# A two-layer trunk with top-2 experts: gates applied at the expert's eviction, and gathers that add into the residual

## The chip, the cores and the metric

One core of one Trainium2 chip. The metric is the device time of one execution in microseconds (us), the median of several runs. The engines are TensorE (PE, matrix products and transpositions), VectorE (DVE), ScalarE (ACT), GpSimd (POOL) and SyncE (SP); transfers run on 16 DMA engines. ACTq, POOLq and SPq are the queues on which ScalarE, GpSimd and SyncE issue their transfers.

## What is computed

The reference is a trunk of two layers on 512 tokens of width 1024, in float32. Layer 0 mixes with a causal convolution, layer 1 with sliding-window attention; both end with a mixture of 16 experts, of which each token takes two. The part that matters here:

```python
def deepnorm(x, sub, g, b):
    return layer_norm(DEEPNORM_ALPHA * x + sub, g, b)

# in grouped_moe: two experts a token, their gates normalised to 1
gate = jnp.take_along_axis(aff, expert, axis=1)
gate = gate / gate.sum(-1, keepdims=True)
...
yb = lax.map(expert_block, (xb, blk_expert)).reshape(P, D)
y = jnp.zeros_like(xt).at[tok_buf].add(yb * gate_buf[:, None].astype(yb.dtype))

# the layer
x = deepnorm(x, mix, ln_g[layer, 0], ln_b[layer, 0])
ffn = grouped_moe(x, router_w, router_b, moe_w_gate[layer], moe_w_up[layer], moe_w_down[layer])
x = deepnorm(x, ffn, ln_g[layer, 1], ln_b[layer, 1])
```

## The kernel before

The 512 tokens are four tiles (T = 4) of 128 rows, held in SBUF as `x_sb`. Each engine has its own program; they meet at semaphores.

**Routing.** For each tile VectorE's `route` chooses two experts and reads their affinities into `gatev`; it signals `s_mask`, and the PE counts ranks (`rank_products`). VectorE's `places` makes of them two row numbers a token (`place_i`, signal `s_place`). After the last tile `table` says how many blocks of 64 rows beyond the first each expert has (`extra`, `s_extra`), and computes all normalised gates, `gate_w`, in three small instructions behind that signal. GpSimd's `scatter(l, t)` (L1507) writes the tile's activations to `xs_dram`, a table of 16 x 512 rows in HBM, with two indirect DMAs of 128 rows of 4 KB. In layer 0 the scatters of tiles 0 and 1 stand in GpSimd's order before the inverse deviations of the normalisation of tiles 2 and 3 (L1570 to L1575); in layer 1 the scatters of tiles 0 and 1 stand behind those of tiles 2 and 3 (L1587 to L1594).

**Experts.** GpSimd waits for all scatters, then fetches 64 rows an expert, four DMAs of 64 KB (`fetch`). The PE runs for each expert e a gate product, an up product, a transposition and a down product, in an order that overlaps e with e - 1 (`step`). SyncE streams the weights, 2 MB each, into six slots; a load waits until the PE has begun the next expert. ScalarE evicts the down product from PSUM with a copy (`store`, L1294) and writes it to `xs_dram`, at the place where the activations were. At the start of the stage ScalarE multiplies `x_sb` by the constant ALPHA (`s_xal`).

**Combine.** GpSimd waits for all stores, and for each tile gathers the two rows of each token (L1561) into two buffers of the tile, `yg[t][0]` and `yg[t][1]`, two indirect DMAs of 512 KB, all eight in one go but for two inverse deviations. ScalarE multiplies the first by its gates (`gated_y`, L1348); VectorE multiplies the second by its gates and adds it to `x_sb` (L1070), adds the first (L1073), and normalises the tile (`norm_x`): moments (L862, L864), subtraction and scale (L882), then, with GpSimd's inverse deviation (`inverse_std`, L1504 and L1505), the rest (L885). VectorE takes tile by tile. In layer 1 the tiles then go to the output.

**Between the layers.** SyncE waits for all eight gathers of layer 0 (L427 and L428) before it loads the two halves of the query weights, then those of the output product, each 2 MB. The PE's first units of attention are the transpositions of tile 0, its KV product, and Q0 and Q1 (L700); VectorE evicts them behind its four normalisations (L1115 to L1126), in its program's order.

The functions `combine` and `scatter` run once a layer. In the convolution stage there is one tile of normalisation after the other, and the routing of a tile follows the normalisation of the next.

## Time and profile before

| | us |
|---|---|
| median of 3 runs | 1238.12 |
| lowest and highest | 1235.01 and 1239.14 |
| the profiled execution | 1231.42 |
| its span in the trace | 1229.8 |

| busy | us | share of the span |
|---|---|---|
| PE | 974.5 | 79% |
| DVE | 493.2 | 40% |
| POOL | 241.2 | 20% |
| ACT | 167.9 | 14% |

In time: the convolution and its routing last to about 312 us, the experts of layer 0 from 324 to 601, the combine of layer 0 from 605 to 642, attention and its routing to about 894, the experts of layer 1 from 908 to 1181, the last combine from 1185 to 1222. In the expert stages the DMA engines are busy nine tenths of the time or more, in the combines the PE is idle.

A busy share is an average over these stages. The order of time (the timeline) shows for each instruction when it starts, how long it takes, and in brackets how long its engine was idle before it and what released it. For a transfer the row is its issue; that it has landed is seen at the instruction that waited for it.

### The profile page before, as it was taken

What the parts mean: (1) busy time and instruction counts of PE and PEld (TensorE: products, weight loads), DVE (VectorE), ACT (ScalarE), POOL (GpSimd) and SP (SyncE); (2) the same over time, 40 slices, a digit from 0 to 9 for tenths busy, and PEclk for the clock granted to TensorE, in tenths of its full rate; (3) what the DMA queues carried; (4) which work ended last, traced back from release to release, by engine and by line L of the source; (5) the groups of instructions that cost most, each with busy time, mean ns of one, the idle gap of its engine ahead of it and who ended that gap; (6) DMA issues with size and microseconds to landing.
All of it is one profiled execution on the core that took longest, in us unless ns stands there. A gap on an engine that the chain in (4) does not pass through costs nothing.

```text
span 1229.8 us, 14566 instructions
## 1 busy us (share of the span) xinstructions
PE 974.5 (79%) x5112; PEld 509.8 (41%) x5113; DVE 493.2 (40%) x967; ACT 167.9 (14%) x375; POOL 241.2 (20%) x335
## 2 busy tenths in 40 slices
PE   5999597996498969899578899967549778999930
PEld 3444243454354435454234454534335334445510
DVE  1799993365211101111185566575511111111126
ACT  0000002120100000000112323433010000000010
POOL 1254500011421202110151002021141121121022
PEclk8999798987699989999888999988769897999975
DMA  9999711025589999999782001300559999999952
GB/s 294 402 402 405 297 69 68 1 103 197 195 322 386 365 385 393 383 341 399 275 289 111 1 1 69 137 1 18 240 195 344 378 393 390 371 399 331 398 183 102
DMA packets 76668, 308.46 MB, mean 251 GB/s; under 512 B 7101, under 2 KB 15465, under 8 KB 68296
## 3 DMA queue, kind: packets, MB, share of 16 engines
q1 hardware_dynamic: 40368, 226.50, 48.5%
q10 hardware_dynamic: 26136, 53.19, 11.6%
q0 software_dynamic: 10112, 28.06, 6.7%
q8 instruction: 34, 0.56, 0.2%
q14 instruction: 18, 0.15, 0.0%
HBM read 252.41 MB, written 55.31 MB: 250 GB/s over the span
## 4 chain that ended last, share of the span: by engine, by line
PE 53%; DMA 21%; DVE 10%; issue 9%; POOL 3%; ACT 2%; SPq 0%; DVEq 0%; ACTq 0%; POOLq 0%
PE ps L581 17%; DMA wring<-in_moe_w_up_dram 9%; PE ps L591 9%; DMA wring<-in_moe_w_gate_dram 8%; PE ps L700 5%; PE ps L526 5%; PE ps L719 5%; PE ps L500 5%; DVE arena L843 2%; DMA wring<-in_conv_w_dram 1%; PE ps L488 1%; DMA xs_dram<-x_sb,place_i 1%; PE ps L745 1%; PE ps L757 1%; POOL vareps L1504 1%
## 5 line engine op out<-in xcount | busy, mean ns | idle before, releaser
L581 PE MATMUL ps<-wring,arena 128*64 128x256 f32 x2624 | 316.1, 398 | 77.0 <-DMA wring<-in_moe_w_gate_dram 32.1
L581 PEld LDWEIGHTS ps<-wring,arena 128*64 128x64 f32 x2624 | 196.5, 144 | 197.8 <-issue 103.1
L1519 POOL DMA_DIRECT2D arena<-xs_dram x172 | 92.0, 535 | 374.4 <-DVE arena L1002 340.3
L591 PE MATMUL ps<-wring,arena 128*64 128x512 f32 x688 | 155.6, 594 | 6.8 <-DVE arena L1037 5.7
L843 DVE SCALAR_TENSOR_TENSOR arena<-arena,dwT 128x512 f32<-128x512 f32 (+1 forms) x174 | 125.4, 798 | 0.0
L488 PE MATMUL ps<-arena,wring 128*128 128x512 f32 x256 | 112.7, 602 | 9.9 <-DMA wring<-in_conv_w_dram 9.6
L1023 DVE COPY arena<-ps 128x256 f32<-128x256 f32 x32 | 13.6, 425 | 258.0 <-PE ps L626 258.0
L700 PE MATMUL ps<-wring,arena 128*128 128x512 f32 x192 | 88.6, 617 | 6.8 <-DMA wring<-in_attn_wq_dram 3.4
L591 PEld LDWEIGHTS ps<-wring,arena 128*64 128x64 f32 x688 | 48.6, 137 | 87.5 <-issue 74.9
L488 PEld LDWEIGHTS ps<-arena,wring 128*128 128x128 f32 x256 | 49.2, 193 | 72.0 <-issue 72.0
L1504 POOL TENSOR_SCALAR vareps<-mv 128x1 f32<-128x1 f32 x20 | 21.2, 1061 | 267.1 <-DVE mv L864 267.0
L500 PE MATMUL ps<-arena,wring 128*128 128x512 f32 x124 | 55.4, 609 | 12.9 <-DVE arena L828 12.9
L526 PE MATMUL ps<-wring,arena 128*128 128x512 f32 x128 | 60.4, 629 | 2.1 <-ACT arena L1255 1.5
L1002 DVE STREAM_TRANSPOSE arena<-arena 128x512 f32<-128x512 f32 x43 | 47.4, 1103 | 33.4 <-DMA arena<-xs_dram 25.7
L719 PE MATMUL ps<-wring,arena 128*128 128x512 f32 x128 | 60.2, 626 | 0.0
L700 PEld LDWEIGHTS ps<-wring,arena 128*128 128x128 f32 x192 | 37.1, 198 | 51.9 <-issue 50.8
L1017 DVE TENSOR_TENSOR arena<-arena,ps 128x256 f32<-128x256 f32 x32 | 13.5, 421 | 101.1 <-PE ps L581 101.1
L1294 ACT ACTIVATE arena<-ps 128x512 f32<-128x512 f32 x32 | 19.1, 597 | 237.7 <-PE ps L591 237.7
L500 PEld LDWEIGHTS ps<-arena,wring 128*128 128x128 f32 x124 | 24.1, 195 | 44.2 <-issue 30.4
L1561 POOL DMA_INDIRECT arena<-xs_dram,place_i x16 | 17.5, 1093 | 119.7 <-DMA xs_dram<-arena 115.7
L1035 DVE TENSOR_TENSOR arena<-arena,ps 128x256 f32<-128x256 f32 x11 | 4.6, 421 | 88.5 <-PE ps L581 88.5
L526 PEld LDWEIGHTS ps<-wring,arena 128*128 128x128 f32 x128 | 25.4, 203 | 32.3 <-issue 30.5
(181 smaller groups left out, 859.1 us busy)
## 6 DMA issues: line engine op xcount, KB each, us to landing
wring<-in_moe_w_up_dram SPq DMA_DIRECT2D x32, 2048.0 KB, 17.5
wring<-in_moe_w_down_dram SPq DMA_DIRECT2D x32, 2048.0 KB, 14.3
wring<-in_moe_w_gate_dram SPq DMA_DIRECT2D x30, 2048.0 KB, 10.2
xs_dram<-zero ACTq DMA_DIRECT2D x1, 32768.0 KB, 105.7
arena<-xs_dram POOLq DMA_DIRECT2D x172, 64.0 KB, 7.3
xs_dram<-arena ACTq DMA_DIRECT2D x86, 128.0 KB, 7.9
wring<-in_conv_w_dram SPq DMA_DIRECT2D x8, 1024.0 KB, 11.4
wring<-in_conv_w_dram SPq DMA_DIRECT2D x2, 2048.0 KB, 17.4
```

Source lines behind the costliest of these rows:

```text
L488: last = pe.matmul(ps[:, 2 * (c % 4) + h, :], w[:, k, h, (c % 2) * P:(c % 2) * P + P], xT[:, k, :], start=(k == 0), stop=(k == KD - 1))
L500: last = pe.matmul(ps[:, 2 * (c % 4) - 4, :], diag(c)[:, k, :], hpad[:, c, k:k + S], start=(k == 0), stop=(k == CW - 1))
L526: last = pe.matmul(ps[:, 4 + h, :], hc[t % 2][:, c, :], slot(4 + c // 4, 4)[:, c % 4, h * 512:(h + 1) * 512], start=(c == 0), stop=(c == K ...
L581: mm = pe.matmul(ps[h * CAP:(h + 1) * CAP, bank, 0:256], act[:, k, :], w[:, k, h * 256:(h + 1) * 256], start=(k == 0), stop=(k == KD - 1))
L591: mm = pe.matmul(ps[h * CAP:(h + 1) * CAP, bank, :], act[:, j % 2, (j // 2) * CAP:(j // 2 + 1) * CAP], w[:, j, h * 512:(h + 1) * 512], sta ...
L700: last = pe.matmul(ps[:, bank, :], xTt[:, k, :], slot(at, KD)[:, k, :], start=(k == 0), stop=(k == KD - 1))
L719: last = pe.matmul(ps[:, bank, :], oT[t % 2][:, k, :], slot(3 + h, KD)[:, k, :], start=(k == 0), stop=(k == KD - 1))
L843: dve.scalar_tensor_tensor(out=acc, in0=hpad[:, one, k:k + S], scalar=dwT[:, one, k:k + 1], in1=acc, op0=ALU.mult, op1=ALU.add).then_inc(s ...
L1002: return dve.transpose(xgT[i].rearrange("p k (h c) -> p h k c", h=2), xg[i].rearrange("p h (c k) -> p h k c", k=KD))
L1294: act.activation(ysb[b], ps[:, 4, :], ACT.Copy).then_inc(s_yc, 1)
L1504: own(pool.tensor_scalar(vareps[:, n:n + 1], mv[:, n, 1:2], EPS, None, ALU.add))
L1519: pool.dma_start(where[q * QROWS:(q + 1) * QROWS, :, :], xs_tiles[q, :, bass.ds(n, 1), :, :]).then_inc(signal, 16)
```

## The change

The gates are applied to the experts' products instead of to the gathered rows. To have them in the order of the places, they are written to a table `gate_dram` of 16 x 512 floats by the same row numbers (two more indirect DMAs a tile, of one float for each of 128 partitions); the table is read back as 128 blocks of 64 twice, side by side (`gate2`), and turned by the PE into `gateT`, with a column for each block. ScalarE's eviction of the down product takes that column as its scale. For the scatters, the gates are normalised tile by tile in `route`.

In the combine, VectorE and ScalarE no longer multiply. For tile 0 the first row's gather adds into `x_sb`, and the second goes to a buffer that VectorE adds. For tiles 1 to 3 both gathers add into `x_sb`, the second issued when the first has landed. SyncE's wait before the query weights counts two gathers for tile 0 and one for each of the others.

```diff
@@ block.sync
             for t in range(T):
-                sp.wait_ge(s_yg[t], 32)
+                sp.wait_ge(s_yg[t], 32 if t == 0 else 16)
@@ block.tensor, experts
                 stage_u(0, 0, 0, False)
+                pe.wait_ge(s_gtab, 32 * (l + 1))
+                pe.transpose(ps[:, 0, 0:P], gate2[:, :, :].rearrange("p h s -> p (h s)"), ident[:, :]).then_inc(s_gT, 1)
                 extras(0, 0, 0)
@@ block.vector, route (and the same for all tiles out of table)
                 own(dve.tensor_reduce(gatev[:, :, t], r3[:, :, :], AX.X, ALU.add))
+                own(dve.tensor_tensor(gsum[:, t:t + 1], gatev[:, 0, t:t + 1], gatev[:, 1, t:t + 1], ALU.add))
+                own(dve.reciprocal(gsum[:, t:t + 1], gsum[:, t:t + 1]))
+                dve.tensor_scalar(gate_w[:, :, t], gatev[:, :, t], gsum[:, t:t + 1], None, ALU.mult).then_inc(s_gw, 1)
@@ block.vector, combine
-                dve.wait_ge(s_xal, T * (l + 1))
+                dve.wait_ge(s_yg[0], 32 * (l + 1))
+                dve.tensor_tensor(x_sb[:, 0, :], x_sb[:, 0, :], y_first, ALU.add).then_inc(s_cmb, 1)
+                dve.wait_ge(s_cmb, l + 1)
                 for t in range(T):
-                    y0, y1 = yg[t]
                     dve.wait_ge(s_yg[t], 32 * (l + 1))
-                    own(dve.scalar_tensor_tensor(out=x_sb[:, t, :], in0=y1, scalar=gate_w[:, 1, t:t + 1],
-                                                 in1=x_sb[:, t, :], op0=ALU.mult, op1=ALU.add))
-                    dve.wait_ge(s_y0g, T * l + t + 1)
-                    dve.tensor_tensor(x_sb[:, t, :], x_sb[:, t, :], y0, ALU.add).then_inc(s_cmb, 1)
-                    dve.wait_ge(s_cmb, T * l + t + 1)
                     norm_x(t, n + t, l, 1)
@@ block.scalar: store (extras alike), experts
-                    act.activation(ysb[b], ps[:, 4, :], ACT.Copy).then_inc(s_yc, 1)
+                    act.activation(ysb[b], ps[:, 4, :], ACT.Copy, scale=gateT[:, bass.ds(e * NBLK, 1)]).then_inc(s_yc, 1)
...
                 silu(0, 0, False)
+                act.wait_ge(s_gT, l + 1)
+                act.activation(gateT[:, :], ps[:, 0, 0:P], ACT.Copy).then_inc(s_gTc, 1)
+                act.wait_ge(s_gTc, l + 1)
...
-            def gated_y(l, t):
-
-                y0 = yg[t][0]
-                act.wait_ge(s_yg[t], 32 * (l + 1))
-                act.activation(y0, y0, ACT.Copy, scale=gate_w[:, 0, t:t + 1]).then_inc(s_y0g, 1)
-
@@ block.gpsimd, scatter
+                if l == 0 and t == 0:
+                    pool.wait_ge(s_ginit, 16)
+                pool.wait_ge(s_gw, T * l + t + 1)
+                for j in range(2):
+                    pool.indirect_dma_start(out=gate_dram[:, :],
+                                            out_offset=bass.IndirectOffsetOnAxis(ap=place_i[:, j, t:t + 1], axis=0),
+                                            in_=gate_w[:, j, t:t + 1], in_offset=None).then_inc(s_gscat, 16)
@@ block.gpsimd, experts
                 gather(1, 1, False)
+                pool.wait_ge(s_gscat, 16 * 2 * T * (l + 1))
+                for h in range(2):
+                    pool.dma_start(gate2[:, h, :], gate_tiles).then_inc(s_gtab, 16)
                 pool.wait_ge(s_extra, l + 1)
@@ block.gpsimd, combine
-                for t in range(T):
-                    for j in range(2):
-                        pool.indirect_dma_start(out=yg[t][j], out_offset=None, in_=xs_dram[:, :],
-                                                in_offset=bass.IndirectOffsetOnAxis(ap=place_i[:, j, t:t + 1], axis=0)
-                                                ).then_inc(s_yg[t], 16)
-                    if t >= 2:
-                        inverse_std(n + t - 2)
-                for t in range(T - 2, T):
-                    inverse_std(n + t)
+                pool.wait_ge(s_xal, T * (l + 1))
+                def collect(t, j, into, how):
+
+                    pool.indirect_dma_start(out=into, out_offset=None, in_=xs_dram[:, :],
+                                            in_offset=bass.IndirectOffsetOnAxis(ap=place_i[:, j, t:t + 1], axis=0),
+                                            compute_op=how).then_inc(s_yg[t], 16)
+
+                collect(0, 0, x_sb[:, 0, :], ALU.add)
+                collect(0, 1, y_first, ALU.bypass)
+                for t in range(1, T):
+                    collect(t, 0, x_sb[:, t, :], ALU.add)
+                for t in range(1, T):
+                    pool.wait_ge(s_yg[t], 32 * l + 16)
+                    collect(t, 1, x_sb[:, t, :], ALU.add)
+                    inverse_std(n + t - 1)
+                inverse_std(n + T - 1)
```

In layer 0 `gate_dram` is set to zero beside `xs_dram`, by one DMA on ScalarE's queue ahead of that one.

## Rows read from the trace of the kernel before

**Rows 1.** The page's chain that ended last, shares of the span by engine.

```profile
PE 53%; DMA 21%; DVE 10%; issue 9%; POOL 3%; ACT 2%; SPq 0%; DVEq 0%; ACTq 0%; POOLq 0%
```

**Rows 2.** Timeline, combine of layer 1: start, us, engine, line, operation [idle before <-releaser].

```profile
1185.04 1.04 POOL L1561 DMA_INDIRECT arena<-xs_dram,place_i  x1 [57.76 <-DMA xs_dram<-arena]
...
1191.38 0.93 POOL L1561 DMA_INDIRECT arena<-xs_dram,place_i  x1 [0.30 <-issue]
...
1191.67 1.28 DVE L1070 SCALAR_TENSOR_TENSOR x_sb<-arena,gate_w,x_sb 128x1024 f32<-128x1024 f32 x1 [14.83 <-DMA arena<-xs_dram,place_i]
...
1197.68 1.15 ACT L1348 ACTIVATE arena<-arena,gate_w 128x1024 f32<-128x1024 f32 x1 [1.35 <-DMA arena<-xs_dram,place_i]
...
1204.96 1.15 ACT L1348 ACTIVATE arena<-arena,gate_w 128x1024 f32<-128x1024 f32 x1 [6.13 <-DMA arena<-xs_dram,place_i]
...
1206.67 1.28 DVE L1070 SCALAR_TENSOR_TENSOR x_sb<-arena,gate_w,x_sb 128x1024 f32<-128x1024 f32 x1
...
1214.13 1.28 DVE L1070 SCALAR_TENSOR_TENSOR x_sb<-arena,gate_w,x_sb 128x1024 f32<-128x1024 f32 x1
...
1220.38 1.28 DVE L885 SCALAR_TENSOR_TENSOR x_sb<-x_sb,rstd,lnrow 128x1024 f32<-128x1024 f32 x1 [0.83 <-POOL rstd L1505]
```

**Rows 3.** Timeline, end of the combine of layer 0 and start of attention.

```profile
621.99 8.88 PE L700 MATMUL ps<-wring,arena 128*128 128x512 f32 x16 [0.73 <-issue]
...
625.42 0.56 SPq L429 DMA_DIRECT2D wring<-in_attn_wq_dram  x1
...
634.25 13.97 PE L700 MATMUL ps<-wring,arena 128*128 128x512 f32 x32 [3.38 <-DMA wring<-in_attn_wq_dram]
...
642.36 0.41 DVE L1115 TENSOR_TENSOR arena<-ps,rows 128x256 f32<-128x256 f32 x1
...
653.64 1.09 PE L712 MATMUL ps<-ident,arena 128*128 128x128 f32 x4 [2.48 <-DVE arena L1096]
```

**Rows 4.** Groups by line, 1180 to 1222 us: count | busy us, mean ns | idle before.

```profile
L1070 DVE SCALAR_TENSOR_TENSOR x_sb<-arena,gate_w,x_sb 128x1024 f32<-128x1024 f32 x4 | 5.1, 1277 | 14.8 <-DMA arena<-xs_dram,place_i 14.8
L1073 DVE TENSOR_TENSOR x_sb<-x_sb,arena 128x1024 f32<-128x1024 f32 x4 | 4.9, 1224 | 0.1
```

**Rows 5.** DMA queues, 600 to 660 us: packets, MB, share of 16 engines' time.

```profile
q0 software_dynamic: 1152, 4.19, 21.4%
```

**Rows 6.** DMA issues of the whole span: size of each, median us to landing.

```profile
arena<-xs_dram POOLq DMA_DIRECT2D x172, 64.0 KB, 7.3
...
x_sb<-in_x_dram SPq DMA_DIRECT2D x4, 512.0 KB, 4.9
lnrow<-in_ln_g_dram ACTq DMA_DIRECT2D x4, 512.0 KB, 10.2
```

**Rows 7.** Timeline, routing of layer 0 and the first expert.

```profile
253.55 0.22 POOL L1504 TENSOR_SCALAR vareps<-mv 128x1 f32<-128x1 f32 x1 [2.92 <-DVE mv L864]
...
288.92 0.17 DVE L948 TENSOR_TENSOR r<-ps,tbase 128x16 f32<-128x16 f32 x1 [9.54 <-PE ps L547]
...
291.43 0.95 POOL L1513 DMA_INDIRECT xs_dram<-x_sb,place_i  x1 [0.30 <-issue]
...
292.60 1.32 POOL L1504 TENSOR_SCALAR vareps<-mv 128x1 f32<-128x1 f32 x1 [0.21 <-DVE mv L864]
...
309.43 0.17 DVE L946 COPY cntf<-ps 128x16 f32<-128x16 f32 x1 [0.30 <-PE ps L551]
...
311.11 0.18 DVE L967 RECIPROCAL gsum<-gsum 128x4 f32<-128x4 f32 x1
...
311.87 0.95 POOL L1513 DMA_INDIRECT xs_dram<-x_sb,place_i  x1 [0.30 <-issue]
...
318.65 4.38 POOL L1519 DMA_DIRECT2D arena<-xs_dram  x8 [5.83 <-DMA xs_dram<-x_sb,place_i]
...
333.39 0.42 DVE L1017 TENSOR_TENSOR arena<-arena,ps 128x256 f32<-128x256 f32 x1 [7.58 <-PE ps L581]
```

**Rows 8.** Timeline, last inverse deviation before the routing of layer 1's last tile.

```profile
876.05 1.32 POOL L1504 TENSOR_SCALAR vareps<-mv 128x1 f32<-128x1 f32 x1 [15.81 <-DVE mv L864]
```

More of the change, by code:

```diff
@@ L137, in trunk @@
         place_i = sb("place_i", [P, 2, T], U32)
+        gate2 = sb("gate2", [P, 2, CAP])
+        gateT = sb("gateT", [P, P])
         cntf = sb("cntf", [P, 2, E])
@@ L190, in trunk @@
         ysb = [view(6912 + i * S, S) for i in range(3)]
-        yg = [[view(at + j * D, D) for j in range(2)] for at in (8448, 8448 + 2 * D, 0, 2 * D)]
+        y_first = view(8448, D)
         spare = view(9472, KD, F)
@@ L273, in trunk @@
         s_xal = sem("s_xal")
-        s_y0g = sem("s_y0g")
         s_cmb = sem("s_cmb")
+        s_ginit = sem("s_ginit")
+        s_gw = sem("s_gw")
+        s_gscat = sem("s_gscat")
+        s_gtab = sem("s_gtab")
+        s_gT = sem("s_gT")
+        s_gTc = sem("s_gTc")
         s_rope = sem("s_rope")
@@ L965, in table @@
                 dve.tensor_copy(extra[:, l, :], more[0:1, :]).then_inc(s_extra, 1)
-                own(dve.tensor_tensor(gsum[:, :], gatev[:, 0, :], gatev[:, 1, :], ALU.add))
-                own(dve.reciprocal(gsum[:, :], gsum[:, :]))
-                dve.tensor_tensor(gate_w[:, :, :], gatev[:, :, :], gsum[:, :].unsqueeze(1).to_broadcast([P, 2, T]),
-                                  ALU.mult)
             dve.wait_ge(s_rows, 16 * 8)
@@ L1305, in extras @@
                             now = act.snap(g, min_val=1, max_val=4096)
-                            row = act.snap(nth, min_val=1, max_val=NBLK - 1) * CAP + e * S
+                            block_of = act.snap(nth, min_val=1, max_val=NBLK - 1) + e * NBLK
+                            row = block_of * CAP
                             act.wait_ge(s_ogate, now)
@@ L1310, in extras @@
                             act.wait_ge(s_oy, now * 32)
-                            act.activation(ysb[2], ps[:, 7, :], ACT.Copy).then_inc(s_oyc, 1)
+                            act.activation(ysb[2], ps[:, 7, :], ACT.Copy,
+                                           scale=gateT[:, bass.ds(block_of, 1)]).then_inc(s_oyc, 1)
                             act.wait_ge(s_oyc, now + 1)
@@ L1342, in experts @@
                 store(E - 1, E // 2 - 1, 1, True)
-            def gated_y(l, t):
-                y0 = yg[t][0]
-                act.wait_ge(s_yg[t], 32 * (l + 1))
-                act.activation(y0, y0, ACT.Copy, scale=gate_w[:, 0, t:t + 1]).then_inc(s_y0g, 1)
             experts(0)
-            for t in range(T - 1):
-                gated_y(0, t)
             def take(u):
@@ L1395, in keep_o @@
                                ACT.Copy).then_inc(s_oT, 1)
-            for i, u in enumerate(first_units):
+            for u in first_units:
                 take(u)
-                if i == 1:
-                    gated_y(0, T - 1)
             for t in range(T):
```

5 lines of the change are left out of this document (3 added, 2 removed).

## The prediction, made before the changed kernel ran

> **What bounds the kernel now.** I read the chain of work that ended last first, by engine [rows 1]: just over half of it is matmuls and a fifth is transfers. Most of that is the two expert stages, which the change hardly touches, and their weight stream follows the PE: an expert's weights are loaded when the PE has left the slot. So whatever starts an expert stage later shifts all behind it, and whatever ends a combine earlier is kept. Three stretches matter: the two combines and the ends of the two routings.
>
> Then I read the order of time in the combine of layer 1 [rows 2]. POOL issues the first gather at 1185.04, and the sixth at 1191.38. VectorE starts tile 0 at 1191.67, when its two rows have landed, and then is bound by its own work: tiles 2 and 3 begin at 1206.67 and 1214.13, 7.46 us apart, and the last normalisation starts at 1220.38 and takes 1.28, so the stage ends at 1221.66, or 36.6 after the first gather. The gathers are not what ends last there: the seventh and eighth are issued behind the first inverse deviation, and tile 3's land at 1204.96 (ScalarE takes them up), 9.2 before VectorE wants them.
>
> Layer 0 is the same until SP comes in [rows 3]: it waits for all eight gathers, issues the query weights at 625.42, and the PE takes them up at 634.25, 8.8 later. VectorE ends its last normalisation at 642.4 and goes straight on to the first key/value eviction, at 642.36. It then does 11.2 us of KV, Q0 and Q1 work, to 653.5, where the PE's last wait for it before the scores ends (653.64). The end of the combine on VectorE is therefore what attention starts from.
>
> **The change, part by part. (a) VectorE in the combine.** Per tile one instruction of 1.277 and one of 1.224 go, with their gaps 1.31 and 1.26 [rows 4]. Tile 0 keeps an addition. That is 4 x 1.31 + 3 x 1.26 = 9.0 us a layer, if VectorE stays the bound. The four ScalarE multiplications end before VectorE needs them in these rows; I cost their removal at nothing.
>
> **(b) What is late next.** The second row of a tile may not be added before the first has landed, and POOL's order is now: five gathers; then for t = 1, 2, 3: wait for tile t's first, issue its second, inverse deviation of tile t-1. So the second gather of tile 3 sits behind the inverse deviation of tile 1, which needs tile 1's second gather landed and its moments. The chain is: first gather of tile 1, second gather of tile 1, moments, inverse deviation, second gather of tile 3, moments, inverse deviation, normalisation. It has landings in it three times, where before there was one.
>
> What an adding gather takes is not in this trace. A plain one: in the window of the first combine the software queue (eight gathers) held 21.4% of the 16 DMA engines' 60 us [rows 5], that is 12.8 / 8 = 1.6 us each. An adding one reads the destination too. Bounds: 1.6 (the second read is hidden) and 3.2 (each row costs as two); below 1.6 is excluded, since all that a plain one does is still done. I take 2.4, the middle, as no row is nearer to either end; the open upper side is a rival. The issue on POOL takes 0.93 and 1.04 in the two rows shown, 1.25 with its gap of 0.30 [rows 2]; I keep that.
>
> The model, in us from the first issue: a gather can start 1.0 after its issue ends, gathers are served one after another, and are seen 1.5 after. For plain ones it gives 6.7 for tile 0 and 13.1 for tile 2; the rows have 6.6 (1191.67) and 12.6 (1197.68, ScalarE) [rows 2]. With 2.4 for adding ones the five first are served by 4.4, 6.0, 8.4, 10.8 and 13.2. Tile 1's first is seen at 9.9, its second is issued at 10.2, queues behind tiles 2 and 3, and is served by 15.6, seen at 17.1. Moments take 1.5 (18.6), the subtraction on VectorE that holds POOL's first instruction 1.3 (19.9), the inverse deviation is ready at 20.6. Tile 3's second is issued at 20.7, served from 22.6 to 25.0, seen at 26.5. Tile 2 keeps VectorE until 26.7; tile 3 then needs 1.5 + 1.3 + 0.7 + 1.3 and ends at 31.6. Against 36.6 that is **5.0 us gained in layer 1**. The same steps give 8.5 gained with 1.6, 0.5 with 3.2, and 4.3 lost with 4.0.
>
> **(c) The combine of layer 0.** SP now waits for tile 0 whole but only for the first gathers of the others. By the model these are all seen at 14.7, at 619.7 instead of 625.4, and 8 MB of weights then run beside the second gathers. The price of that for a landing is between 0 (the second gathers go first) and 10.2 - 4.9 = 5.3, the difference between 512 KB loads beside other traffic and 512 KB loads at the start [rows 6]. I take 2 for tiles 2 and 3 and 1 for tile 1 (half of it is through by then), nearer to 0, because the rows with 10.2 ran beside expert weights in rows of 16 KB, while these are rows of 2 KB. The stage ends at 34.4 instead of 31.6. Before it ended at 642.4 - 605.0 = 37.4; **gain 3.0**, with bounds from 5.8 (price 0) to a loss of 1.9 (price 5.3).
>
> The Trainium skill, page "DMA: Bandwidth & Descriptors", section on queues, rings and completion order, says that a DMA engine changes between queues at whole packets. By that a gather of 4 KB rows among short packets would at most double in service, 2.4 instead of my 2; no row here shows it for these sizes.
>
> The weights arrive 5.7 sooner, at 634.25 - 5.7 = 628.5 or a little later; the PE finishes its KV product at 630.9 (621.99 + 8.88), so Q0 and Q1, 13.97 together, run from 631 to 645, and VectorE ends Q1 at about 650, against 653.5. The gain of 3.0 passes; no more than 5.0 could.
>
> **(d) Routing, layer 0** [rows 7]. Each scatter of a tile is followed by two more indirect DMAs of one gate per partition. The row count is the same as for the activations, so I take the same 1.25 each, 2.5 a tile. They stand before an inverse deviation that VectorE waits for. At tile 1's scatter the second activation scatter runs from 291.43 to 292.38, and the inverse deviation's first instruction starts at 292.60, 0.2 later, and takes 1.32. With 2.5 more it starts at 295.0, 2.4 later. By then VectorE's subtraction is over and I let it take 0.22, as at 253.55, 1.1 less: **1.3 lost**. The same at tile 0's scatter ends in a stretch of 9.5 us in which VectorE waits for the PE, before 288.92: nothing. The three gate instructions that moved from the table into the routing take 0.2 each (the reciprocal 0.18). Of the 0.6, 0.30 lies in VectorE's wait for the rank product before 309.43: **0.3 lost**. The last tile's gate scatters are issued behind the last activation scatter (311.87), while POOL waits for that until 318.65: hidden.
>
> **(e) The gate table.** Two loads of 64 floats a partition on POOL behind the eight fetches that start at 318.65: 2 x 0.55, the price of a fetch, so issued by 324.1. They land by 331.5, if they take the 7.3 of the median fetch, most of them beside weights [rows 6]. The PE ends its first up product at 333.4, where VectorE takes it up, so the wait is covered by 2 us; without that cover each microsecond later would be a microsecond on the path. What stays is a 128 x 128 transposition in the PE's order before expert 1: **0.3 lost**. ScalarE's copy of it and POOL's fetches for expert 2, 1.1 later, lie under the PE's product for expert 1.
>
> **(f) Evictions with a gate per partition.** Same instruction, 32 + 11 times, hidden behind the PE except the last of a layer: 0 to 0.2, I take **0.1**.
>
> **(g) Layer 1.** The tail of routing (0.3), the transposition (0.3) and the last eviction (0.1) repeat; the gate scatters stand before no inverse deviation that is waited for, since POOL is idle for 15.8 us before the last one, at 876.05 [rows 8]. In attention each routing on VectorE grows by 0.6 and one of three lies on the chain; between 0 and 1.7, I take **0.6**.
>
> The losses: 1.3 + 0.3 + 0.3 + 0.1 + 0.3 + 0.3 + 0.1 + 0.6 = 3.3. The sum: 5.0 + 3.0 - 3.3 = **4.7 us gained**. The profiled execution has 1231.42 (span 1229.8), and would go to 1226.7. The median of the three runs, 1238.12, lies 6.7 above it; I take the gain off that: 1233.4.
>
> **The rivals.** *1. An adding row costs as two* (3.2 us a gather). For it: two reads for each row written. Against: a plain gather keeps an engine only partly busy with data. Layer 1 gains 0.5, layer 0 loses 1.7 (the model with the same prices of 2 and 1), the rest loses 3.3: 4.5 lost, 1242.6. The Trainium skill, page "Collectives: The Full Stack", section on the bandwidth ceiling, states for the adding step of a reduce that it takes two read descriptors for a chunk on one ring and moves at about half the rate of a copy; by that it would be this rival. No row here shows an adding transfer.
>
> *2. The other side: the added gathers become the bound.* The mechanism is the queue of adding gathers on the software ring: at 4.0 us or more each, the five first ones alone take 17.6 us, tile 1's second is seen at 25, and the chain through tile 3's gives 4.3 lost in layer 1, 6.5 in layer 0, 14 lost with the rest: 1252. It decides from about 3.3 us a gather in layer 1 and 2.8 in layer 0. For it: the chain has three landings where one was covered. Against: there are only seven adding gathers a layer.
>
> *3. Adding is nearly free* (1.6). Layer 1 gains 8.5, layer 0 its cap of 5.0, 10.2 gained: 1228.
>
> *4. Contention in layer 0 at its full price* (5.3) with 2.4 a gather: layer 0 loses 1.9, the sum is 0.2 lost: 1238.3.
>
> **Chances.** Forecast 0.30, rival 1 0.25, rival 2 0.20, rival 3 0.15, rival 4 0.10. The predicted time is 1233. About 0.3%, 3.7 us, is what a measurement can tell from no change. Faster by more: rival 3 and nine tenths of the forecast, 0.42. Slower by more: rival 2, and about six tenths of rival 1, 0.35. Within: the rest, 0.23. The range for eight in ten reaches from 1225 (rival 3 with cheaper routing, 13 gained) to 1254 (rival 2). The forecast's own range is 1228 to 1238.
>
> **What would show it.** The landing of an adding gather: tile 1's first is issued at 2.5 and its second at 10.2 in the forecast; VectorE idle before its moments, not busy in one piece; the end of the combine 31.6 after the first gather; SP's query weights at about 15 after it; the inverse deviation of the fourth tile in layer 0 at 0.22 instead of 1.32 and 2.4 later; no wait of the PE before the transposition of the gates. I am wrong if the issue of an adding gather on POOL takes much more than 0.95, if gate scatters of 4 bytes land so slowly that the table comes after the first up product, or if the added gathers are served at another rate than 1.6 to 3.2.

## The result, and where the time went

| | before | after |
|---|---|---|
| median, us | 1238.63 (1235.01 to 1239.61, 4 runs) | 1251.12 (1250.09 to 1255.94, 4 runs) |
| span of the profiled execution | 1229.8 | 1248.5 |

The medians differ by 12.5 us, which is 1.0%. The ratio over the runs is 1.0135 with an interval of 1.0098 to 1.0171: the changed kernel is slower by 1.0% to 1.7%, or 12 to 21 us. The spans of the two profiled executions, on which the stretches below rest, differ by 18.7. The forecast was 4.7 us faster.

The page of the kernel after: first the busy time of each engine (us, share, instructions), then the software queue's packets, MB and share of 16 engines' time.

```profile
PE 975.1 (78%) x5114; PEld 508.9 (41%) x5115; DVE 479.5 (38%) x971; ACT 163.1 (13%) x369; POOL 264.3 (21%) x355
...
q0 software_dynamic: 10752, 28.20, 8.7%
```

The PE has the same work (975.1 against 974.5) and VectorE 13.7 us less, as meant. POOL has 23.1 more. The gain is in the busy time and not in the span, so the time went into waits. The milestones of the two timelines say into which. "First fetch" is POOL's first L1527 of a layer (L1519 before), "first gather" its first L1573 (L1561), "combine" lasts from there to the end of VectorE's fourth L897 (L885), and attention from there to the first moments (L874, L862) of the last tile ahead of the routing of layer 1.

| stretch | before | after | difference | forecast |
|---|---|---|---|---|
| start to first fetch, layer 0 | 318.7 | 325.5 | +6.9 | +1.6 |
| experts, layer 0, to the first gather | 286.4 | 290.4 | +4.0 | +0.4 |
| combine, layer 0 | 37.4 | 38.6 | +1.2 | -3.0 |
| attention | 232.0 | 230.2 | -1.8 | +0.6 |
| end of attention to first fetch, layer 1 | 28.1 | 37.4 | +9.3 | +0.3 |
| experts, layer 1 | 282.6 | 283.4 | +0.8 | +0.4 |
| combine, layer 1 | 36.6 | 34.6 | -2.0 | -5.0 |

Two rows carry the loss, 16.2 of 18.4 us: each is the end of a routing. POOL in layer 0 (start us, duration us, engine, line, operation, count, and in brackets the idle time before and what ended it):

```profile
292.58 1.97 POOL L1521 DMA_INDIRECT gate_dram<-gate_w,place_i  x1 [0.30 <-issue]
294.85 0.96 POOL L1521 DMA_INDIRECT gate_dram<-gate_w,place_i  x1 [0.30 <-issue]
295.83 0.25 POOL L1505 TENSOR_SCALAR vareps<-mv 128x1 f32<-128x1 f32 x1
...
313.20 0.96 POOL L1514 DMA_INDIRECT xs_dram<-x_sb,place_i  x1 [2.25 <-DVE place_i L971]
314.46 0.96 POOL L1514 DMA_INDIRECT xs_dram<-x_sb,place_i  x1 [0.30 <-issue]
...
325.51 4.36 POOL L1527 DMA_DIRECT2D arena<-xs_dram  x8 [7.56 <-DMA xs_dram<-x_sb,place_i]
```

The rows of before that answer to these are in [rows 7]. The last activation scatter is issued at 314.46, 2.6 later than before (311.87). But the fetch comes 11.05 after it, where it came 6.78 after it before: 4.3 more, and what ends the wait is the landing of the activation scatters. The same in layer 1, after and then before:

```profile
904.84 0.96 POOL L1514 DMA_INDIRECT xs_dram<-x_sb,place_i  x1 [0.30 <-issue]
...
922.06 4.36 POOL L1527 DMA_DIRECT2D arena<-xs_dram  x8 [13.72 <-DMA xs_dram<-x_sb,place_i]
```

```profile
894.25 0.95 POOL L1513 DMA_INDIRECT xs_dram<-x_sb,place_i  x1 [0.30 <-issue]
902.49 4.36 POOL L1519 DMA_DIRECT2D arena<-xs_dram  x8 [7.28 <-DMA xs_dram<-x_sb,place_i]
```

17.2 us from issue to fetch against 8.2: 9.0 more. The activation scatters are the same; what is new on their queue are the gate scatters between them. The software queue in the stretch ahead of the fetch (packets, MB, share of 16 engines' time), after from 908 to 922 us, then before from 888 to 902:

```profile
q0 software_dynamic: 634, 1.81, 64.3%
```

```profile
q0 software_dynamic: 738, 2.63, 46.0%
```

After, it was busy for 9.0 us of the 14 and moved 1.81 MB, 201 GB/s of its busy time; before 6.4 us and 2.63 MB, 408 GB/s. Something in the queue holds engines and brings no bytes. (The two windows lie differently to the scatters; the whole stretch follows with f4 below.)

The last combine after, in the same columns:

```profile
1205.46 1.72 POOL L1573 DMA_INDIRECT x_sb<-xs_dram,place_i  x1 [57.85 <-DMA xs_dram<-arena]
...
1208.79 1.56 POOL L1573 DMA_INDIRECT x_sb<-xs_dram,place_i  x1 [0.30 <-issue]
...
1216.87 1.53 POOL L1573 DMA_INDIRECT x_sb<-xs_dram,place_i  x1 [2.82 <-DMA x_sb<-xs_dram,place_i]
...
1224.10 1.28 DVE L874 BATCH_NORM_STATS2 bns<-x_sb 128x6 f32<-128x512 f32 x2 [3.29 <-DMA x_sb<-xs_dram,place_i]
...
1227.87 1.65 POOL L1573 DMA_INDIRECT x_sb<-xs_dram,place_i  x1 [0.19 <-issue]
...
1235.10 1.29 DVE L874 BATCH_NORM_STATS2 bns<-x_sb 128x6 f32<-128x512 f32 x2 [1.11 <-DMA x_sb<-xs_dram,place_i]
...
1238.79 1.28 DVE L897 SCALAR_TENSOR_TENSOR x_sb<-x_sb,rstd,lnrow 128x1024 f32<-128x1024 f32 x1 [0.83 <-POOL rstd L1506]
```

Against [rows 2]: VectorE was busy in one piece there; here it waits for landings, 3.29 before tile 1 and 1.11 before tile 3. The chain runs as forecast, through the second gather of tile 1 (11.4 after the first issue) and that of tile 3 (22.4), but 34.6 long. An adding gather takes POOL 1.53 to 1.65, where a plain one takes 0.93 and 1.04 [rows 2].

Layer 0, against [rows 3]:

```profile
615.86 1.74 POOL L1573 DMA_INDIRECT x_sb<-xs_dram,place_i  x1 [58.04 <-DMA xs_dram<-arena]
...
632.78 0.56 SPq L439 DMA_DIRECT2D wring<-in_attn_wq_dram  x1
...
635.99 1.29 DVE L874 BATCH_NORM_STATS2 bns<-x_sb 128x6 f32<-128x512 f32 x2 [3.38 <-DMA x_sb<-xs_dram,place_i]
...
639.76 1.67 POOL L1573 DMA_INDIRECT x_sb<-xs_dram,place_i  x1 [0.19 <-issue]
...
648.72 1.29 DVE L874 BATCH_NORM_STATS2 bns<-x_sb 128x6 f32<-128x512 f32 x2 [2.82 <-DMA x_sb<-xs_dram,place_i]
...
652.15 7.11 PE L712 MATMUL ps<-wring,arena 128*128 128x512 f32 x16 [0.62 <-DMA wring<-in_attn_wq_dram]
...
652.38 2.12 DVE L897 SCALAR_TENSOR_TENSOR x_sb<-x_sb,rstd,lnrow 128x1024 f32<-128x1024 f32 x1 [0.82 <-POOL rstd L1506]
```

Tile 3's second gather takes 9.0 from its issue (639.76) to VectorE, beside the query weights; in layer 1 it took 7.2. The stage is 38.6 long, 4.0 more than in layer 1: tile 1 comes 1.5 later (20.1 after the first issue, 18.6 there), tile 3's landing costs 1.7 more, and the last normalisation takes 2.12, 0.8 more, while POOL runs a 128x1024 instruction beside it.

### The profile page after: what moved, and what is told of

Same layout as the page of the kernel before. It is cut to its first block, busy times and chain, and to the rows that moved or that the text cites. A ratio compares the mean times of both kernels' runs of the same rounds, so it can differ in the third digit from the quotient of the medians.

```text
span 1248.5 us, 14615 instructions
## 1 busy us (share of the span) xinstructions
PE 975.1 (78%) x5114; PEld 508.9 (41%) x5115; DVE 479.5 (38%) x971; ACT 163.1 (13%) x369; POOL 264.3 (21%) x355
## 4 chain that ended last, share of the span: by engine, by line
PE 52%; DMA 25%; issue 9%; DVE 8%; ACT 2%; POOL 2%; SPq 0%; DVEq 0%; ACTq 0%; POOLq 0%
PE ps L591 17%; DMA wring<-in_moe_w_up_dram 8%; PE ps L601 8%; DMA wring<-in_moe_w_gate_dram 8%; PE ps L712 5%; PE ps L536 5%; PE ps L510 4%; PE ps L731 4%; DMA x_sb<-xs_dram,place_i 4%; DMA xs_dram<-x_sb,place_i 2%; DVE arena L855 2%; DMA wring<-in_conv_w_dram 1%; PE ps L498 1%; PE ps L769 1%; PE ps L783 1%
## 5 line engine op out<-in xcount | busy, mean ns | idle before, releaser
L1527 POOL DMA_DIRECT2D arena<-xs_dram x172 | 92.0, 536 | 384.8 <-DVE arena L1013 344.0
L712 PE MATMUL ps<-wring,arena 128*128 128x512 f32 x192 | 86.8, 605 | 4.1 <-ACT arena L1370 2.7
L601 PEld LDWEIGHTS ps<-wring,arena 128*64 128x64 f32 x688 | 48.6, 137 | 87.8 <-issue 75.1
L1013 DVE STREAM_TRANSPOSE arena<-arena 128x512 f32<-128x512 f32 x43 | 47.4, 1102 | 47.7 <-DMA arena<-xs_dram 39.9
L712 PEld LDWEIGHTS ps<-wring,arena 128*128 128x128 f32 x192 | 36.3, 194 | 48.1 <-issue 47.0
L1302 ACT ACTIVATE arena<-ps,gateT 128x512 f32<-128x512 f32 x32 | 22.0, 687 | 242.8 <-PE ps L601 242.8
L1573 POOL DMA_INDIRECT x_sb<-xs_dram,place_i x14 | 23.1, 1650 | 124.8 <-DMA xs_dram<-arena 115.9
## 6 DMA issues: line engine op xcount, KB each, us to landing
xs_dram<-arena ACTq DMA_DIRECT2D x86, 128.0 KB, 7.9
```

Source lines behind the costliest of these rows:

```text
L601: mm = pe.matmul(ps[h * CAP:(h + 1) * CAP, bank, :], act[:, j % 2, (j // 2) * CAP:(j // 2 + 1) * CAP], w[:, j, h * 512:(h + 1) * 512], sta ...
L712: last = pe.matmul(ps[:, bank, :], xTt[:, k, :], slot(at, KD)[:, k, :], start=(k == 0), stop=(k == KD - 1))
L1013: return dve.transpose(xgT[i].rearrange("p k (h c) -> p h k c", h=2), xg[i].rearrange("p h (c k) -> p h k c", k=KD))
L1302: act.activation(ysb[b], ps[:, 4, :], ACT.Copy, scale=gateT[:, bass.ds(e * NBLK, 1)]).then_inc(s_yc, 1)
L1527: pool.dma_start(where[q * QROWS:(q + 1) * QROWS, :, :], xs_tiles[q, :, bass.ds(n, 1), :, :]).then_inc(signal, 16)
L1573: pool.indirect_dma_start(out=into, out_offset=None, in_=xs_dram[:, :], in_offset=bass.IndirectOffsetOnAxis(ap=place_i[:, j, t:t + 1], axi ...
```

## The experiments

**The change in two halves.** Theory A: the gate path costs the time (gate scatters ahead of and among the activation scatters). Rival B: the combine with its adding gathers costs it. e1 keeps the gates and puts the old combine back:

```diff
-                    collect(t, 0, x_sb[:, t, :], ALU.add)
...
-                    collect(t, 1, x_sb[:, t, :], ALU.add)
+                for t in range(T):
+                    for j in range(2):
+                        pool.indirect_dma_start(out=yg[t][j], out_offset=None, in_=xs_dram[:, :],
...
+                    own(dve.tensor_tensor(x_sb[:, t, :], x_sb[:, t, :], y1, ALU.add))
+                    dve.tensor_tensor(x_sb[:, t, :], x_sb[:, t, :], y0, ALU.add).then_inc(s_cmb, 1)
```

> The gate table, its scatters and the scaled evictions stay; the combine is again eight plain gathers, with two additions on VectorE and nothing on ScalarE (the same result as the reference). Theory A, the gate scatters hold back the activation scatters behind them: routing is as late as in the changed kernel (last activation scatter seen 10.8 us after its issue in layer 0 and 17 in layer 1, against 6.5 and 8 before), the combines last 37 us as before, and the time is that of the changed kernel or a little above, 1251 to 1254. Theory B, the adding gathers are the cost: 1238 to 1241.

Measured: 1251.31, ratio 1.0159 (1.0126 to 1.0192): all of the loss is there without one adding gather. First fetch at 325.1 in layer 0, 10.5 after the last activation scatter, and 15.4 after it in layer 1. The combines are those of before (37.4 and 36.3). A holds.

e2 keeps the new combine and leaves the gates out of the eviction:

```diff
-                pool.wait_ge(s_gw, T * l + t + 1)
-                for j in range(2):
-                    pool.indirect_dma_start(out=gate_dram[:, :],
...
-                    act.activation(ysb[b], ps[:, 4, :], ACT.Copy, scale=gateT[:, bass.ds(e * NBLK, 1)]).then_inc(s_yc, 1)
+                    act.activation(ysb[b], ps[:, 4, :], ACT.Copy).then_inc(s_yc, 1)
```

> The adding gathers stay; the gate table, its scatters, its transposition and the scale at the eviction are left out, so the experts' products are added without their gates. Theory A: routing is as before the change, layer 0's combine 38.6 us and layer 1's 34.6 as in the changed kernel, and the time is 1235 to 1239. Theory B: 1248 to 1252.

Measured: 1248.54, ratio 1.0121 (1.0088 to 1.0154). The time can't be used: without gates other values reach layer 1, its tokens are routed otherwise, and an expert needs one more block (44 transpositions of fetched rows, L1011, where the kernel after has 43, L1013), 11 to 12 us of that stage. I hadn't seen that coming, and the expected time missed by it. The milestones of layer 0, where the data are still the same, can be used: first fetch at 318.6, as before. So the adding gathers have no part in the late fetch. Its combines are 40.0 and 35.1 long, those of after 38.6 and 34.6.

**Size or something else?** e3 writes rows of 512 bytes instead of 4, to a table that nobody reads:

```diff
+    wide_dram = nc.dram_tensor("wide_dram", [E * S, 128], F32).ap()
...
-                    pool.indirect_dma_start(out=gate_dram[:, :],
+                    pool.indirect_dma_start(out=wide_dram[:, :],
...
-                                            in_=gate_w[:, j, t:t + 1], in_offset=None).then_inc(s_gscat, 16)
+                                            in_=zero[:, 0:128], in_offset=None).then_inc(s_gscat, 16)
```

> The changed kernel with its gate scatters made of rows of 512 B instead of 4 B, written to a table of their own that nobody reads; the gate table that is read stays zero, so the experts' products are left out of the sum. Same number of indirect DMAs and of rows. Theory A1, it is the 4-byte size of the writes that holds the queue: the last activation scatter is seen about 7 us after its issue in layer 0 and 9 to 10 in layer 1, and the time is 1240 to 1244. Theory A2, each row costs a turn of its engine whatever its size: 10.8 and 17 stay, 1251.

Measured: 1248.29, ratio 1.0121 (1.009 to 1.0152), with the same extra block as e2, so again its time can't be used. But from the last activation scatter to the fetch it has 5.8 in layer 0 and 8.2 in layer 1, against 11.05 and 17.2 after: 128 times the bytes, and the delay is gone.

**SP.** e4 lets SP wait for every gather before the query weights, as the kernel before does:

```diff
-                sp.wait_ge(s_yg[t], 32 if t == 0 else 16)
+                sp.wait_ge(s_yg[t], 32)
```

> The changed kernel, but SyncE waits for both gathers of every tile before it loads the query weights, as before the change. Theory C, the weights beside the second gathers cost layer 0 its gain: the combine of layer 0 falls from 38.6 us to 35 to 36 us, but the query weights come 7 us later than now, so attention begins no sooner; the time within 2 us of the changed kernel's 1251. Rival, the adding gathers alone are the cost of that stage: it stays at 38.6 and the time rises by 5.

Measured: 1261.56, ratio 1.0253 (1.0222 to 1.0284), 10 us above the median of after, and not within 2 as I had expected. The combine of layer 0 is shorter, 35.3, so the weights did slow the gathers by about 3. But the weights then come late: they are issued 29.6 us after the first gather instead of 16.9, and the PE stands 10.26 before Q0 (L712). Its last wait for VectorE before the scores (L724) ends 58.5 us after the first gather, where it ends 49.9 in the kernel after and 50.0 in its repetition e5: 8.5 later. So with this order of gathers the earlier load was the right side of the trade. The traced execution is the fastest of e4's six, 7 below its median; what the others lose beyond this no trace shows.

**The gate scatters alone.** The next four kernels are the kernel before with nothing added but two scatters a tile to a table that nobody reads, so their data and their routing are those of before. f1 has the rows of after, 4 bytes at the token's place:

```diff
+    side = nc.dram_tensor("side", [E * S, 1], F32).ap()
...
+                for j in range(2):
+                    pool.indirect_dma_start(out=side[:, :],
+                                            out_offset=bass.IndirectOffsetOnAxis(ap=place_i[:, j, t:t + 1], axis=0),
+                                            in_=half[:, :], in_offset=None).then_inc(s_gscat, 16)
...
+                pool.wait_ge(s_gscat, 16 * 2 * T * (l + 1))
```

> The kernel before with nothing but two more indirect DMAs behind each tile's activation scatters: one float for each of 128 partitions, by the same row numbers, to a table that nobody reads; GpSimd waits for them before the second expert's extras. Theory A (the 4-byte rows hold back the activation scatters behind them): from the last normalisation before routing to the first fetch, layer 1 takes 37 us against 28 before, the last activation scatter of layer 0 is seen 10 to 11 us after its issue against 6.5, and the time is 14 to 17 us above the kernel before. Rival (they are harmless, the gates' other work on VectorE and the PE costs the time): no more than 4 us above.

f2 writes 512 bytes a row instead (`side` with 128 columns, from `zero[:, 0:128]`):

> As f1, with 512 B for each partition in place of 4 B. Theory A1 (the size or the crowding of the small writes is the cost): layer 1's routing takes 28 to 29 us, layer 0's last activation scatter is seen within 7.5 us, and only the 2 to 3 us of issue before an inverse deviation in layer 0 remain: 2 to 4 us above the kernel before. Theory A2 (128 more rows in the queue, whatever their size): as f1.

f3 writes 4 bytes a row, but rows that lie 512 bytes apart:

```diff
+    side = nc.dram_tensor("side", [E * S * 128, 1], F32).ap()
...
+                dve.tensor_scalar(place_s[:, :, t], placef[:, :], 128.0, None, ALU.mult)
...
+                                            out_offset=bass.IndirectOffsetOnAxis(ap=place_s[:, j, t:t + 1], axis=0),
```

> As f1, with 4 B for each partition, but with the rows 512 B apart in the table (one small instruction more on VectorE makes the row numbers). Theory A1a, it is crowding (neighbouring tokens of an expert write neighbouring floats): as f2, 2 to 4 us above. Theory A1b, it is the size of each write alone: as f1, 14 to 17 us above.

f4 is f3 with 64 bytes from row to row (16.0 instead of 128.0):

> As f3 (the kernel before with extra 4-byte scatters to a table nobody reads), with the rows 64 B apart instead of 512 B. If writes disturb each other only within 64 B: as f3, within 4 us of the kernel before, and the first fetch of layer 0 about 6 us after the last activation scatter's issue. If they do within 512 B: between f1 and f3, the fetch 8 to 12 us after.

| added to the kernel before | ratio | last activation scatter to first fetch, layer 0 | layer 1 |
|---|---|---|---|
| nothing | 1 | 6.8 | 8.2 |
| f1: 4 B rows, side by side | 1.0181 (1.0132 to 1.023) | 12.4 | 19.5 |
| f2: 512 B rows | 1.0051 (1.002 to 1.0083) | 5.5 | 10.8 |
| f3: 4 B rows, 512 B apart | 1.0024 (0.9997 to 1.0052) | 5.8 | 10.5 |
| f4: 4 B rows, 64 B apart | 1.0061 (1.0032 to 1.0089) | 5.6 | 10.8 |

f1 and then f4, POOL at the end of layer 1's routing:

```profile
911.70 0.96 POOL L1516 DMA_INDIRECT xs_dram<-x_sb,place_i  x1 [0.30 <-issue]
912.97 0.97 POOL L1520 DMA_INDIRECT side<-half,place_i  x1 [0.30 <-issue]
914.24 0.97 POOL L1520 DMA_INDIRECT side<-half,place_i  x1 [0.30 <-issue]
931.22 4.36 POOL L1526 DMA_DIRECT2D arena<-xs_dram  x8 [16.01 <-issue]
```

```profile
897.36 0.96 POOL L1518 DMA_INDIRECT xs_dram<-x_sb,place_i  x1 [0.30 <-issue]
898.62 0.96 POOL L1522 DMA_INDIRECT side<-half,place_s  x1 [0.30 <-issue]
899.89 0.96 POOL L1522 DMA_INDIRECT side<-half,place_s  x1 [0.30 <-issue]
908.20 4.35 POOL L1528 DMA_DIRECT2D arena<-xs_dram  x8 [7.35 <-issue]
```

Same issues, same durations, same number of rows, same bytes; only the addresses differ, and the wait falls from 16.01 to 7.35. f4's software queue from 897 to 908 us:

```profile
q0 software_dynamic: 808, 2.20, 50.1%
```

That is 2.20 MB in 5.5 us of busy time, 399 GB/s, again what the kernel before has (408). For the whole stretch of layer 1's scatters, first before (873 to 903 us), then after (884 to 922), the queue has:

```profile
q0 software_dynamic: 864, 3.15, 25.6%
```

```profile
q0 software_dynamic: 1056, 3.15, 35.1%
```

The same 3.15 MB take 7.7 us of the 16 engines before and 13.3 after; with f1 (897 to 931) it is 13.3 and with f4 (883 to 908) 7.8. The single packets in the traces show which ones grew. The packets of the small rows take under 0.02 us each on the mean. The 768 packets of 4 KB of the activation scatters take 0.159 us each before and in f4, but 0.273 on the mean after and 0.272 in f1, where about 110 of them take more than 0.4. What the small rows cost is thus paid by the large rows that share their queue.

So neither the size of a row nor the number of rows costs the time, but where the floats are written: the places of an expert's tokens are consecutive, so in f1 they lie 4 bytes apart, in f4 64. Distances between the two were not tried. With the distance the table grows from 32 KB to 512 KB, and whether the nearness of two floats counts or the smallness of the whole table was not separated either, nor which tile's gate scatters do it. That this happens where a piece of memory is written again before its last write is through is an argument and wasn't measured.

The Trainium skill, page "DMA: Bandwidth & Descriptors", section Specifications, says that below 512 bytes a transfer becomes a read-modify-write. By that rule f3 and f4 would be as slow as f1. The trace agrees only for neighbours: 4 byte rows 64 bytes apart wait 10.8, like rows of 512 bytes.

What f2 to f4 still cost is 0.2% to 0.6%. A part is the issue of the scatters: the first fetch of layer 0 comes at 320.3 to 320.4 instead of 318.65. In layer 1 it is not the landing: by the semaphore events the last activation scatter has landed 7.9 to 8.2 us after its issue, as before (7.95), and in f1 16.9 after it, as in the kernel after (16.9). In all four POOL then stands another 2.64 us before the fetch, where it stands 0.29 in the kernels before and after, and the profile names no releaser (`issue`); its cause is open. It is the same in f1 and f4, so their difference of 8.7 is all landing.

f1 is 22 us slower than before by the ratio, and 30 us by the spans of the traced executions. Of these its two routings take 7.2 and 11.3. The rest lies in the experts of layer 0 (3.5) and in attention (6.6), and the next run shows how much these differ without any change.

**After once more**, beside these on their chip:

> The changed kernel once more, unaltered, beside f1 to f3. Theory A: 12 to 18 us above the kernel before, and within 3 us of f1, because its combines give back about as much in layer 1 as they cost in layer 0. Theory B (the combine is the loss): f1 is well below it.

Measured: 1251.18, ratio 1.0111 (1.0064 to 1.0158). In its trace the experts of layer 0 take 287.6 and attention 238.4, where the first trace of the same kernel has 290.4 and 230.2. With the same gate table, e1, e4 and e7 have 285.3 to 285.8 in the experts of layer 0, and before has 286.4, so the +4.0 in the table above is no effect of the change. Over all traces with the right data attention lies between 230.2 and 240.4, so a single trace can't tell a few us there. The late fetches are another matter: every trace with the floats side by side has them, 10.5 to 12.4 us after the last activation scatter in layer 0 and 15.4 to 19.5 in layer 1, and no other has more than 6.9 and 10.8.

**What adding costs.** e6 is after with gathers that overwrite:

```diff
-                    collect(t, 0, x_sb[:, t, :], ALU.add)
+                    collect(t, 0, x_sb[:, t, :], ALU.bypass)
...
-                    collect(t, 1, x_sb[:, t, :], ALU.add)
+                    collect(t, 1, x_sb[:, t, :], ALU.bypass)
```

> The changed kernel with all its gathers plain: they overwrite the residual instead of adding to it, so the residual and one of the two products of a token are left out, and layer 1 routes other tokens; only the combines are compared. Order, waits and bytes are those of the changed kernel. If the price is the adding itself (issue 1.55 us against 0.95, service 2.8 us against 1.6): the combine of layer 1 falls from 34.6 us to 27 to 29 us, and eight gathers take 13 us of the DMA engines instead of 21. If it is the dependent chain of second gathers alone: it stays above 32.

Measured, in a single execution: 1268.11; layer 1 gets other data here, and only lengths are read. Its last combine, and the software queue from 600 to 660 us:

```profile
1230.19 1.03 POOL L1573 DMA_INDIRECT x_sb<-xs_dram,place_i  x1 [65.50 <-DMA xs_dram<-arena]
...
1232.79 0.94 POOL L1573 DMA_INDIRECT x_sb<-xs_dram,place_i  x1 [0.30 <-issue]
...
1256.75 1.28 DVE L897 SCALAR_TENSOR_TENSOR x_sb<-x_sb,rstd,lnrow 128x1024 f32<-128x1024 f32 x1 [0.83 <-POOL rstd L1506]
```

```profile
q0 software_dynamic: 1152, 4.19, 20.3%
```

The combine takes 27.8 in layer 1 and 31.8 in layer 0, 6.8 and 6.9 less than after. The order of the change is good: in layer 1 it would gain 8.8 on the kernel before. The addition in the transfer takes 6.8 of that back. In the same window the kernel after has 36.5%: 21.9 us of service against 12.2, 9.7 more for seven adding gathers. That is 1.4 each on top of 1.5, so 2.9; layer 1 gives 2.8 (48.6% of the 44 us from 1203 to 1247, less 1.6 for the plain one, over 7). On POOL it is 1.55 instead of 0.95.

**Without the wait between the two rows of a tile.** e7 adds only the first row in the transfer and the second on VectorE, with all gathers issued at once:

```diff
-                    pool.wait_ge(s_yg[t], 32 * l + 16)
-                    collect(t, 1, x_sb[:, t, :], ALU.add)
+                    collect(t, 1, yg[t], ALU.bypass)
...
+                    dve.tensor_tensor(x_sb[:, t, :], x_sb[:, t, :], yg[t], ALU.add).then_inc(s_cmb, 1)
```

> The changed kernel, but in every tile only the first gather adds into the residual and the second goes to a buffer that VectorE adds; all eight are issued in one go, none waits for another, and SyncE waits for all. Same result as the reference. By the measured 2.8 us for an adding and 1.6 us for a plain gather the tiles land every 4.4 us, and VectorE is the bound at 6.15 us a tile: both combines last 33 to 34.5 us (38.6 and 34.6 in the changed kernel, 37.4 and 36.6 before), and the time is 2 to 5 us below the changed kernel's. If adding gathers are slowed by each other in the queue beyond that, 36 us or more.

Measured: 1248.98, ratio 1.0124 (1.0074 to 1.0175): not told from after. The combines are 35.6 and 34.9, where I had expected 33 to 34.5. VectorE is the bound again, from the second tile on; in the first it waits 1.91 for its inverse deviation instead of 0.84, since POOL is still issuing gathers.

```profile
1211.77 1.23 DVE L1079 TENSOR_TENSOR x_sb<-x_sb,arena 128x1024 f32<-128x1024 f32 x1 [17.58 <-DMA arena<-xs_dram,place_i]
...
1218.98 1.22 DVE L1079 TENSOR_TENSOR x_sb<-x_sb,arena 128x1024 f32<-128x1024 f32 x1
...
1225.12 1.22 DVE L1079 TENSOR_TENSOR x_sb<-x_sb,arena 128x1024 f32<-128x1024 f32 x1
```

**A version without the loss.** v2 has the gate table with 64 bytes from row to row, read back whole and picked by ScalarE; the gates normalised behind the places; in layer 0 the gate scatters of the first two tiles behind the inverse deviations; and in the combine e7's order for layer 0 and the first two tiles of layer 1, adding gathers for the other two.

```diff
+PITCH = 16
...
+    gate_dram = nc.dram_tensor("gate_dram", [E * S * PITCH, 1], F32).ap()
...
+                                            out_offset=bass.IndirectOffsetOnAxis(ap=place_s[:, j, t:t + 1], axis=0),
...
+                    last = act.activation(gate2[:, h, :], gate_in[h][:, 0::PITCH], ACT.Copy)
...
+                if l == 1 or t >= 2:
+                    scatter_gates(l, t)
...
+                    if l == 0 or t < 2:
+                        collect(t, 1, yg[t], ALU.bypass)
```

> A version of the change made of what the runs showed: the gate table has one float in 64 B, is read back whole and picked out by ScalarE; the gates are normalised behind the signal of the places instead of in front of it, and in layer 0 the gate scatters of tiles 0 and 1 stand behind the inverse deviation; in the combine every tile's first gather adds, and VectorE adds the second, except for tiles 2 and 3 of layer 1, where both gathers add. Same result as the reference. If crowding within 64 B was the cost: routing as before in both layers, combines of 34 and 32.5 us, 3 to 7 us below the kernel before. If the crowding reaches further than 64 B: 3 to 12 us above it.

Measured: 1230.34 against 1233.40, ratio 0.9978 (0.995 to 1.0005), 12 runs. It is well below the kernel after (the versions with the floats side by side are at 1.011 to 1.016, and e4 at 1.025) and not shown to be faster than the kernel before: the interval reaches 1, and 2.7 us by the ratio is less than the 3 to 7 that I had expected. It changes several things at once, so their shares can be read from the stretches only.

```profile
312.50 0.95 POOL L1524 DMA_INDIRECT xs_dram<-x_sb,place_i  x1 [0.30 <-issue]
...
317.86 4.36 POOL L1541 DMA_DIRECT2D arena<-xs_dram  x8 [1.86 <-DMA xs_dram<-x_sb,place_i]
...
896.84 0.95 POOL L1524 DMA_INDIRECT xs_dram<-x_sb,place_i  x1 [0.30 <-issue]
...
905.68 4.36 POOL L1541 DMA_DIRECT2D arena<-xs_dram  x8 [5.35 <-DMA xs_dram<-x_sb,place_i]
...
1189.69 1.72 POOL L1587 DMA_INDIRECT x_sb<-xs_dram,place_i  x1 [57.90 <-DMA xs_dram<-arena]
...
1221.58 1.28 DVE L901 SCALAR_TENSOR_TENSOR x_sb<-x_sb,rstd,lnrow 128x1024 f32<-128x1024 f32 x1 [0.83 <-POOL rstd L1516]
```

The fetches come 5.4 and 8.8 after the last activation scatter, and the combines take 35.3 and 33.2: 2.2 and 3.4 less than before. The idea of the change is then worth 5.6 us in the combines, by one trace of each.

## Why the prediction was wrong, step by step

- **(d), the routings: the step that failed.** It said that the last tile's gate scatters are hidden while POOL waits for the activation scatters, and it priced a gate scatter by POOL's issue alone, since the row count is that of an activation scatter. It gave no price to what the rows do in the queue on which POOL's wait ends. In layer 0 that is 4.3 us, and 9.0 in layer 1, where (g) put the gate scatters at nothing because they stand before no inverse deviation that is waited for. f1 shows this cost alone. The prediction did name "gate scatters of 4 bytes land so slowly" as a way to be wrong, but for the table only; the table was never late. No rival had this mechanism.
- The issue part of (d) held in kind: the inverse deviation shrank to 0.25 (0.22 expected). Its size was 2.6 instead of 1.6; one of the 16 gate scatters took 1.97 instead of 0.95. The lines of [rows 7] show no such issue; in the kernel before the eighth gather of each combine takes 1.9.
- **(b), the price of an adding gather.** The chain through tile 3's second gather was right, and so was the model: tile 1's second was issued at 11.4 (10.2 expected), tile 3's at 22.4 (20.7), its rows were seen at 29.6 (26.5), the end was 34.6 (31.6). The mis-sized term is 2.4 for an adding gather, measured 2.8, and its issue, 1.55 instead of 0.95. So 2.0 were gained instead of 5.0. The 2.8 lies midway between the forecast and rival 1 (3.2), and the gain nearer to the rival's 0.5; the rival's total of 1242.6 was still 8.5 too low for want of (d).
- The page that rival 1 names, the Trainium skill's "Collectives: The Full Stack", section on the bandwidth ceiling, puts an adding step at about half the rate of a copy. The trace nearly agrees: 2.8 against the 1.57 of a plain gather in the last combine before, 1.8 times.
- **(c), layer 0.** SP's weights went out at 16.9 (14.7 expected), and the prices for their contention were good: 1.7 measured for the 2 on tile 3, and 1.5 for the 1 on tile 1. What was missing is what layer 1 lacks too (3.0, by the 0.4 more per adding gather and its issue), 0.5 of tile 1, and 0.8 in the last normalisation. Lost 1.2, where 3.0 were to be gained. That attention starts from the end of the combine held only just: the second half of the query weights arrived at 652.15, as late as the last tile. Attention was 1.8 shorter, within what one trace differs from the next.
- **(a), (e), (f), and the rest of (g).** VectorE's busy time fell as meant; the transposition took 0.33 (0.3) with its table there in time; the evictions went from 0.60 to 0.69. From the end of attention to the last activation scatter of layer 1 it takes 0.3 more (0.3 expected). These were right. The 0.6 for attention can't be told, since attention differs by more from trace to trace.
- **Rival 2** ended near the measured time (1252) with the wrong mechanism: adding gathers of 4 us. The time lies within the range of 1225 to 1254 by luck: the range reached that far for the sake of rival 2, and what filled it is the cost of the gate scatters.

Open: why attention differs by 8 us between two executions of one kernel (230.2 and 238.4), what in the memory makes neighbouring floats slow, and how far apart they must lie.

## What to carry to other kernels

A small transfer has two prices, its issue and what it does to the queue that it joins: where a wait ends on that queue, look for small scattered rows that lie side by side, and try them further apart; 64 bytes were enough here. An addition in a transfer removes VectorE's instruction but made the transfer 1.8 times and its issue 1.6 times as long here; on the chain it gave back 6.8 of 8.8 us. Before a part of a computation is left out for an experiment, ask whether the data steer later work.

## What the runs showed of the hardware

- Indirect scatters of 4 byte rows to neighbouring addresses held back the scatters beside them by 6.9 and 8.7 us (f1 against f4), and the 4 KB packets of these took 0.272 us instead of 0.159 in layer 1; at 64 bytes from row to row they cost the same as rows of 512 bytes (5.6 and 10.8 us against 5.5 and 10.8).
- An indirect gather of 128 rows of 4 KB that adds into SBUF takes 2.8 to 2.9 us of the 16 DMA engines instead of 1.5 to 1.6 (after against e6 and before), and mostly 1.55 us on POOL instead of 0.95.
- The issue of an indirect scatter of 128 rows takes 0.96 us on POOL, by the median, whether a row has 4 bytes, 512 bytes or 4 KB (f1, f2); one small scatter in 16 took 1.96 to 1.97 in each of f1, f2 and the kernel after.
